# A two-block transformer kernel on one core: a last tile that ends in narrower parts, a norm turned by a diagonal, stand-in products, and an output step moved

## The reference

```python
def rms_norm_2(x, g):
    y = xf * lax.rsqrt(jnp.mean(xf * xf, axis=-1, keepdims=True) + EPS)
    return (y * g.astype(jnp.float32)).astype(x.dtype)
...
def second_block(x, c, ...):
    sh1, sc1, ga1, sh2, sc2, ga2 = jnp.split(mod, 6, axis=-1)
    for _ in range(DEPTH_2):                # DEPTH_2 = 1
        h = modulate(rms_norm_2(x, g_attn), sh1, sc1)
        x = x + ga1[:, None, :] * hybrid_mixer(h, w_in, b_f, sinks, w_out)
        h2 = modulate(rms_norm_2(x, g_mlp), sh2, sc2)
        x = x + ga2[:, None, :] * conv_glu_mlp(h2, w_up, conv_w, conv_b, w_down)
    return rms_norm_2(x, g_final)
```

## Time and profile before

| | us |
|---|---|
| median of three runs | 1611.72 |
| lowest and highest | 1610.78, 1612.98 |
| the profiled execution | 1614.05 |
| its span, first to last instruction | 1612.3 |
| TensorE matmuls busy in it | 1368.0 |
| mean granted TensorE clock | 0.927 of 2.4 GHz |

### The profile page before, as it was taken

One profiled execution on the slowest core, in us unless ns is written; L12 is line 12 of the kernel. 1 busy time (PEld: TensorE's weight loads), 2 busy tenths in 40 slices (PEclk: granted clock), 3 DMA queues, 4 the chain that ended last, 5 costly groups with the idle time before them and its releaser, 6 DMA issues.

```text
span 1612.3 us, 24352 instructions
## 1 busy us (share of the span) xinstructions
PE 1368.0 (85%) x9392; PEld 823.7 (51%) x9392; DVE 561.5 (35%) x1481; ACT 263.1 (16%) x736; POOL 103.6 (6%) x191
## 2 busy tenths in 40 slices
PE   9989998776776877989998768767668999999998
PEld 4445554443433433555654434334335876888843
DVE  3444633221221223552532212212213043577721
ACT  2143211010010011453110100100101133111100
POOL 1312000000000001310100000000001041000000
PEclk9999999898898899999999877988988979999999
DMA  8877999999999999636999999999999621644300
GB/s 295 309 269 278 395 402 421 421 421 422 422 422 422 422 422 391 239 131 239 417 411 420 420 420 420 421 420 420 421 421 353 220 79 42 206 157 155 133 0 26
DMA packets 117190, 512.99 MB, mean 318 GB/s; under 512 B 11872, under 2 KB 46620, under 8 KB 64872
## 3 DMA queue, kind: packets, MB, share of 16 engines
q1 hardware_dynamic: 115376, 507.49, 79.5%
q0 software_dynamic: 1552, 4.06, 0.8%
q10 hardware_dynamic: 168, 0.09, 0.0%
HBM read 510.54 MB, written 1.07 MB: 317 GB/s over the span
## 4 chain that ended last, share of the span: by engine, by line
PE 35%; DMA 12%; SPq 7%; DVE 2%; issue 1%; ACT 1%; POOL 0%; POOLq 0%; DVEq 0%; ACTq 0%
PE bank L2176 9%; DMA ring<-in_moe_w_up 7%; SPq L1634 7%; PE bank L2208 5%; PE bank L1226 4%; DMA BC<-in_moe_w_up 3%; PE bank L1931 3%; PE bank L397 2%; PE bank L409 2%; DMA BC<-in_moe_w_gate 2%; PE bank L1213 1%; PE bank L1241 1%; PE bank L645 1%; PE bank L668 1%; PE bank L502 1%; PE bank L1254 1%
## 5 line engine op out<-in xcount | busy, mean ns | idle before, releaser
L1226 PE MATMUL bank<-ring,hT 128*32 128x256 f32 (+1 forms) x2976 | 304.2, 465 | 153.2 <-DMA ring<-in_moe_w_up 61.0
L1226 PEld LDWEIGHTS bank<-ring,hT 128*32 128x32 f32 (+1 forms) x2976 | 154.9, 134 | 271.2 <-issue 164.1
L1226 PE MATMUL bank<-BC,hT 128*32 128x256 f32 (+1 forms) x1120 | 166.2, 461 | 50.4 <-DMA ring<-in_moe_w_up 26.9
L1485 DVE TENSOR_SCALAR pT<-pT 128x256 f32<-128x256 f32 x34 | 10.0, 294 | 465.5 <-ACT pT L1601 465.5
L2176 PE MATMUL bank<-hT,ring 128*128 128x256 f32 (+1 forms) x768 | 153.0, 362 | 0.0
L2176 PEld LDWEIGHTS bank<-hT,ring 128*128 128x128 f32 x768 | 136.0, 190 | 16.6
L1226 PEld LDWEIGHTS bank<-BC,hT 128*32 128x32 f32 (+1 forms) x1120 | 81.2, 134 | 90.7 <-issue 64.8
L1213 PE MATMUL bank<-A,hn 128*128 128x128 f32 x1088 | 127.2, 275 | 0.0
L502 PE MATMUL bank<-ring,hT 128*128 128x512 f32 (+4 forms) x352 | 123.1, 511 | 4.0 <-DVE hT L300 2.5
L1213 PEld LDWEIGHTS bank<-A,hn 128*128 128x128 f32 x1088 | 124.5, 192 | 1.7 <-issue 1.7
L1254 PE MATMUL bank<-hT,A 128*128 128x512 f32 x256 | 118.4, 605 | 0.0
(11 more groups left out here) (300 smaller groups left out, 1484.8 us busy)
## 6 DMA issues: line engine op xcount, KB each, us to landing
ring<-in_moe_w_up SPq DMA_DIRECT2D x98, 1024.0 KB, 26.6
ring<-in_moe_w_down SPq DMA_DIRECT2D x96, 1024.0 KB, 26.5
ring<-in_moe_w_gate SPq DMA_DIRECT2D x88, 1024.0 KB, 25.7
BC<-in_moe_w_gate SPq DMA_DIRECT2D x40, 1024.0 KB, 24.7
BC<-in_moe_w_up SPq DMA_DIRECT2D x30, 1024.0 KB, 24.1
BC<-in_moe_w_down SPq DMA_DIRECT2D x28, 1024.0 KB, 27.1
ring<-in_w_ada SPq DMA_DIRECT2D x24, 1024.0 KB, 6.7
ring<-in_w_up SPq DMA_DIRECT2D x22, 1024.0 KB, 5.3
```

Source lines behind the costliest of these rows:

```text
L1226: i = nc.tensor.matmul(GATE[q * cap:(q + 1) * cap, part * FF:(part + 1) * FF], xg[:, c, q * cap:(q + 1) * cap], u[:, c, :], start=(c == 0) ...
```

## The change

Four edits.

- The last tile. Tile 1's down product now goes into three parts: 512 columns, then 256, then 256 (in bank 0). Behind each part DVE multiplies by the gate, adds to X, and multiplies the new X by g_final into hn while the root is not there yet. ACT squares 768 columns and then the last 256 (tile 0: 512 and 512); POOL adds both sums in its first instruction; DVE multiplies hn by the root in two halves; SP sends the first half of the tile and ACT the second.
- The norms n3 and n4. DVE no longer scales a whole tile: it scales the 128x128 identity by the roots (into modrow), and PE turns X by a real matmul against that diagonal.
- The third mixer's start. Two matmuls of 512 columns on constants, whose output nobody reads, stand before the turn of tile 0 and two more behind it (keep_warm).
- The first attention's output product: the two pieces of item 8 move behind item 10's transposes of heads.

```diff
@@ norm_stage
             def scale(dve, tt):
-                tile_ready(dve, tt)
                 dve.wait_ge(*rooted(tt + 1))
-                nc.vector.tensor_scalar(hn[:, tt, :], X[:, tt, :], rstd[:, tt:tt + 1], None,
-                                        ALU.mult).then_inc(scaled.sem, 1)
+                nc.vector.tensor_scalar(diagonal_of(tt), ident, rstd[:, tt:tt + 1], None, ALU.mult).then_inc(scaled.sem, 1)
...
+                    if late_root:
+                        i = nc.tensor.transpose(dst, X[:, tt, c:D:DC], ident)
+                    else:
+                        i = nc.tensor.matmul(dst, X[:, tt, c:D:DC], diagonal_of(tt), start=True, stop=True)
@@ close_tensor_short (warm=True for n3 alone)
+            if warm:
+                keep_warm(pe, 7, NB, 2)
             norm.turn(pe, 0)
+            if warm:
+                keep_warm(pe, 7, NB, 2)
+        def keep_warm(pe, b, width, times=1):
+            for _ in range(times):
+                nc.tensor.matmul(bank[b][:, 0:width], ident, konst[:, P:P + width], start=True, stop=True)
@@ OutStage.tensor
-                    counts = (2, 2, 0, 2, 2, 2, 1, 1)
+                    counts = (0, 2, 2, 2, 2, 2, 1, 1)
@@ mlp_tensor
+        parts_of = [[(bank[4], 0, NB), (bank[5], NB, D)],
+                    [(bank[6], 0, NB), (bank[7][:, 0:256], NB, 768), (bank[0][:, 0:256], 768, D)]]
...
+            for tt, together in ((0, parts_of[0]), (1, parts_of[1][0:1]), (1, parts_of[1][1:2]), (1, parts_of[1][2:3])):
@@ mlp_vector
+                    dv.done(nc.vector.tensor_tensor(product, ps, gate_rows[1][:, a:b], ALU.mult))
+                    nc.vector.tensor_tensor(xs, xs, product, ALU.add).then_inc(out_added.sem, 1)
+                    done += 1
+                    dve.wait_ge(*out_added(done))
+                    dv.done(nc.vector.tensor_tensor(hn[:, tt, a:b], xs, g_fin[:, a:b], ALU.mult))
@@ last_scalar
+            for tt, added, a, b in ((0, 1, 0, NB), (0, 2, NB, D), (1, 4, 0, 768), (1, 5, 768, D)):
+                act.wait_ge(*out_added(added))
+                nc.scalar.activation(square_at[:, a:b], X[:, tt, a:b], ACT.Square,
+                                     accum_out=last_ss[:, tt, (a > 0) * 1:(a > 0) * 1 + 1]).then_inc(last_sq.sem, 1)
+            act.wait_ge(*result(4))
+            act.dma_start(out[0, P:S, NB:D], hn[:, 1, NB:D]).then_inc(final_out.sem, 16)
@@ last_scale
+            for n in range(2):
+                y = hn[:, tt, n * NB:(n + 1) * NB]
+                nc.vector.tensor_scalar(y, y, r, D ** 0.5, ALU.mult, ALU.mult).then_inc(result.sem, 1)
@@ sync engine
+            sp.wait_ge(*result(3))
+            sp.dma_start(out[0, P:S, 0:NB], hn[:, 1, 0:NB]).then_inc(final_out.sem, 16)
```

More of the change, by code:

```diff
@@ L249, in norm_stage, with diagonal_of @@
         def norm_stage(tile_ready, gain, shift=None, extra=(), late_root=False):
+            def diagonal_of(tt):
+                return modrow[:, tt * P:(tt + 1) * P]
             st = Stage()
@@ L279, in turn @@
                     pe.wait_ge(*scaled(tt + 1))
-                rows = X if late_root else hn
+                    tile_ready(pe, tt)
                 for c in range(DC):
-                    i = nc.tensor.transpose(bank[4 + 2 * tt + c // 4][:, (c % 4) * P:(c % 4 + 1) * P],
-                                            rows[:, tt, c:D:DC], ident)
+                    dst = bank[4 + 2 * tt + c // 4][:, (c % 4) * P:(c % 4 + 1) * P]
+                    if late_root:
+                        i = nc.tensor.transpose(dst, X[:, tt, c:D:DC], ident)
+                    else:
+                        i = nc.tensor.matmul(dst, X[:, tt, c:D:DC], diagonal_of(tt), start=True, stop=True)
                 i.then_inc(turned.sem, 1)
@@ L342, in close_vector_late, with close_tensor_short @@
             norm.evac(dve, 1, 0)
-        def close_tensor_short(pe, products, norm):
+        def close_tensor_short(pe, products, norm, warm=False):
             for tt in range(TT):
@@ L2196, in mlp_tensor @@
             pe.wait_ge(*cw_out(1))
[L2198 to L2211, removed]
+            for tt, together in ((0, parts_of[0]), (1, parts_of[1][0:1]), (1, parts_of[1][1:2]), (1, parts_of[1][2:3])):
+                for j in range(PAIRS):
+                    u = down_units[j]
+                    if tt == 0:
+                        pe.wait_ge(*hid3(j + 1))
+                        unit_here(pe, u)
+                    w = units[u][0](slot(u))
+                    for c in range(2):
+                        for ps, a, b in together:
+                            i = nc.tensor.matmul(ps, hidT3[:, 2 * j + c, tt * P:(tt + 1) * P], w[:, c, a:b],
+                                                 start=(j == 0 and c == 0), stop=(j == PAIRS - 1 and c == 1))
+                i.then_inc(down_done.sem, 1)
         def mlp_scalar(act):
@@ L2255, in mlp_vector @@
             dve.wait_ge(*fin_in(16))
+            done = 0
             for tt in range(TT):
-                for n in range(2):
-                    dve.wait_ge(*down_done(tt * (n + 1) + 1))
-                    gated(1)(tt, n, bank[4 + 2 * tt + n][:, :]).then_inc(out_added.sem, 1)
+                for k, (ps, a, b) in enumerate(parts_of[tt]):
+                    dve.wait_ge(*down_done(1 if tt == 0 else 2 + k))
+                    xs, product = X[:, tt, a:b], BC[:, 7168 + a:7168 + b]
+                    dv.done(nc.vector.tensor_tensor(product, ps, gate_rows[1][:, a:b], ALU.mult))
[3 more added lines that the diff above has]
+                    dv.done(nc.vector.tensor_tensor(hn[:, tt, a:b], xs, g_fin[:, a:b], ALU.mult))
@@ L2260, in mlp_vector @@
                 last_scale(dve, tt)
-        last_sq, last_rs, result = shared("sum_sq", 2), shared("sum_rs", 2), sem("result")
+        last_sq, last_rs, result = shared("sum_sq", 4), shared("sum_rs", 2), sem("result")
+        last_ss = stat[:, 0:4].rearrange("p (t k) -> p t k", t=TT)
+        square_at = A[:, 2048:2048 + D]
         def last_scalar(act):
[L2266 to L2269, removed]
+            for tt, added, a, b in ((0, 1, 0, NB), (0, 2, NB, D), (1, 4, 0, 768), (1, 5, 768, D)):
[4 more added lines that the diff above has]
+            act.dma_start(out[0, P:S, NB:D], hn[:, 1, NB:D]).then_inc(final_out.sem, 16)
@@ L2298, in _ @@
             load(m2_units[1], len(units))
[L2299 to L2302, removed]
+            sp.wait_ge(*result(2))
+            sp.dma_start(out[0, 0:P, :], hn[:, 0, :]).then_inc(final_out.sem, 16)
+            sp.wait_ge(*result(3))
+            sp.dma_start(out[0, P:S, 0:NB], hn[:, 1, 0:NB]).then_inc(final_out.sem, 16)
+            sp.wait_ge(*final_out(16 * 3))
         @block.gpsimd
```

15 lines of the change are left out of this document (7 added, 8 removed).

## The result

| | before | after |
|---|---|---|
| median, us | 1610.19 (6 runs) | 1618.24 (6 runs) |
| lowest and highest | 1608.05, 1612.98 | 1616.45, 1621.96 |
| the profiled execution | 1614.05 | 1621.96 |
| its span | 1612.3 | 1620.1 |
| TensorE matmuls busy in it | 1368.0 | 1383.4 |

A forecast was written before the change was run, and what follows sets the result against it. TensorE, busy 1368.0 of 1612.3 us, was taken to bound the kernel, with an unoverlapped tail behind it. Tail -2.0, n4 +1.8, n3 -1.4 and first attention +0.2 gave -1.4 us: 1610.3 us, range 1607.6 to 1613.1.

The forecast's parts named there:

- The price of a turn: n4: 16 real-matmul instructions at 0.112 us take 1.79 us against 0.88 for eight transposes, 0.91 more for each turn.
- The bounds I gave: n4's two turns: +1.6 if a turn's start is hidden, +2.2 us if a hand-over is exposed at each turn.
- the sum of -1.4: Whole kernel: tail -2.0, n4 +1.8, n3 -1.4 and first attention +0.2 make -1.4 us.
- n4: +1.8 forecast: n4's two turns lie in TensorE's gapless run, so their longer real matmuls are paid in full: +1.8 us.
- n3: -1.4 forecast: Third mixer's start: faster matmuls at full clock, half given back to longer turns and tile 1's root: -1.4 us.
- The credit for the clock: n3: with idle time filled the clock stays at 1.00, twelve matmuls take 2.6 us instead of 5.4.
- The rival with the short fall: n3: without a profile before's clock fall is short, so n3 is worth -0.1 us, giving 1611.6; chance 0.15.
- The first attention: +0.2 forecast: Item 8 without the pieces: TensorE idles about 0.25 us longer awaiting ACT's copy, same work at half clock: +0.2 us.
- a second one comes: First attention's upper bound: a second half-clock stretch, since the pieces no longer cover item 8's hand-over to ACT: +1.6 us.
- The tail: -2.0 forecast: Behind the last matmul: narrower steps, smaller square, split final scaling and two transfers save 2.0 us.
- The rival that gave this to ACT's queue: Tail: ACT's transfer as late as the whole tile was, tail only -1.0 us, 1611.3 in all; chance 0.10.
- The rival for slower by over 3.2 us: Whole kernel: several rivals at once and a stall not seen here, slower by over 3.2 us; chance 0.03.

The follow-up runs named there:

- the last tile alone: Before with only the new last tile (512 + 256 + 256 columns, early g_final, two halves out), also called the tail alone: 1609.49 us, 1.0002.
- the turn alone: Before with only the real matmul against the diagonal of roots in n3 and n4, nothing else of the change: 1618.31 us, 1.0054.
- stand-ins alone: Before with only the four keep_warm matmuls on constants around n3's first turn, transposes kept: 1610.46 us, 1.0000.
- the turn with contiguous columns: Before with only the real-matmul turn, reading 128 neighbouring columns of X (computes another function): 1611.12 us, 1.0008.
- four kernels with the same last steps: New last tile on before: by itself 1.0002, with keep_warm 0.9998, all edits but the real-matmul turn 0.9991, the latter with SP sending both halves 0.9985.

## Why the prediction failed

**The price of a turn: the step that failed.** For n4, "real products of 128 columns are two instructions each, and 32 of those take 3.57 us, 0.112 each: 16 take 1.79". The two instructions are right, and the 0.112 is right for the earlier trace rows, whose stationary operand lies without gaps. The turn's stationary operand is X at every eighth element. In before's turns the operand has the same gaps, and there eight transposes take 0.88 us with loads of 0.188 to 0.191 us. The data is what these load, too: a weight load's shape in the trace is that of the transposed data and not that of the identity, as in the turn of 44x128 rows against an identity of 44x44 (L2171). And before's transposes of contiguous columns (L656) load faster than its gapped ones:

```profile
L656 PEld LDWEIGHTS bank<-konst,BC x96: 137/141/230, 100.8 to 1354.5; 128*128 128x128 f32 x96
L2171 PEld LDWEIGHTS bank<-konst,BC x4: 136/138/139, 1374.7 to 1374.8; 44*128 44x128 f32 x4
L2171 PE MATMUL bank<-konst,BC x4: 232/233/256, 1374.7 to 1374.9; 44*128 44x44 f32 x4
```

So the gapped slice is the stationary operand before and after. A transpose's load takes 0.141 us without gaps and 0.188 with them; a real matmul's takes 0.192 without and 0.336 with. Why the gaps cost the real matmul 0.144 us and the transpose 0.047 no run here tells. But that they cost something at all stood in the trace of before. The bounds I gave, +1.6 to +2.2, had both been taken within this one reading of the row, so the range couldn't hold what came. No row that the forecast used has a gapped stationary operand in a real matmul; the price was therefore unknown, and was treated as known to 0.2 us for each turn.

Put the measured turns, 3.87, 4.03, 3.69 and 3.82 us, in place of the forecast's 1.8, 1.8, 1.79 and 1.79, and the sum of -1.4 becomes -1.4 + 15.4 - 7.2 = +6.8. The spans of the profiled executions differ by +7.8, the medians by +8.05. One term was mis-sized, and it entered four times.

**n4: +1.8 forecast, +5.7 measured.** The mechanism was right: both turns lie in TensorE's gapless run, and every microsecond arrived at the end. With contiguous columns the turns took exactly what was forecast.

**n3: -1.4 forecast, +2.7 measured.** Three of its steps came: the granted clock stays at 1.00 in every kernel that has the stand-ins, the twelve matmuls take 2.91 us (2.6 forecast), and the second turn's first load waits for tile 1's root. The two turns add 4.3 us to what was forecast, and -1.4 + 4.3 = +2.9 meets the measured +2.7 to 0.2. The credit for the clock, though, was the price of one execution. Before's fall at n3 lasts 6.8 us, that of the last tile alone, which idles the same, 3.4, and with the turn alone TensorE idles 1.49 and 1.71 us and the clock doesn't fall at all. So against the turn alone the stand-ins gave after nothing, and against before their ratio alone is 1.0000. The rival with the short fall, at 0.15, had the right idea of this. Where no fall would have come, the stand-ins should cost about nothing, by the rows: from the end of the last product to the first turn it is 2.04 us with them and 2.03 without, to the twelve matmuls 4.90 and 4.89 (stand-ins alone against before). That is an estimate; no execution with transposes, without stand-ins and without a fall was seen.

**The first attention: +0.2 forecast, +1.2 in the profiled execution, nothing that can be told in the ratio.** The wait is 2.42 us and not 2.14, and is ended by ACT's copy, as forecast; after's row:

```profile
120.50 1.22 PE L681 MATMUL bank<-A,pT 128*128 128x128 f32 x4 [2.42 <-ACT pT L792]
```

What made it 1.2 is the clock, in after for 6.8 us instead of 3.4 (before: the earlier trace rows):

```profile
118.00:120.50 2.50, 0.09 (x2) 0.01 (x1) 1.31 (x7) 1.30 (x5) 0.73 (x2) 0.95 1.01 419
120.50:127.00 6.50, 6.50 (x16) 3.56 (x17) 2.51 (x9) 2.86 (x13) 1.48 (x5) 0.50 1.01 425
```

But before and eight of the kernels, with the moved pieces or without, show a fall of 3.4 us there, and the turn alone and the turn with contiguous columns, whose first attention is before's to the instruction and idles the same 2.14 us, show none; the row of the turn alone for 118 to 128:

```profile
118.00:128.00 10.00, 8.22 (x40) 4.80 (x40) 5.51 (x23) 5.80 (x24) 2.31 (x6) 1.00 1.01 424
```

So the same program there has a fall in one execution and none in another, and the moved pieces have one of 6.8 us in after and of 3.4 in four other kernels: the length of a fall goes with the execution and not with the edit. The bound of "a second one comes" was +1.6, and 1.2 lies in it.

**The tail: -2.0 forecast, -1.75 measured, -0.8 in four kernels with the same last steps.** The steps in DVE, ACT and POOL are what was forecast to 0.1 us (0.42, 0.42, a square of 0.42, 0.88 for both halves), and 6.23 us against the "about 6.0" named ahead. The term that varies is the landing of the second half: 2.2 us were taken (0.4 less than the big transfer's 2.6), and it came to 2.3 in after and to 3.2 where the thin rest comes. The rival that gave this to ACT's queue was near in the size for the kernels with the rest (-1.0 against -0.8), not for after, and wrong in the cause. Neither size shows in the ratios of the tail alone, 1.0002 ± 0.0012: an edit of 0.8 to 1.75 us is below what 12 runs tell here.

**The sign.** The rival for slower by over 3.2 us stood at 0.03 as "several of these at once and a stall not seen here". It should have been one mechanism with a price, and much of what it needed was in the trace: all four turns of n3 and n4 are on the chain, and the gapped loads took 0.188 us where contiguous ones took 0.141. The point from which it decides was near. From -1.4 to +3.2 it is 4.6 us, 1.15 for each turn, 0.072 for each of its 16 instructions: at 0.184 us for one and not 0.112 the change is slower by over 0.2%. It came to 0.24.

## What to carry to other kernels

A duration taken from another row is only as good as its operands' access: before a transpose is replaced by a real matmul, look at how far apart the columns of the stationary operand lie, for a gap that costs a transpose's weight load little (0.047 us here) can cost a real matmul's three times as much and set the pace. Where an edit repeats on the critical path, the widest bound belongs to its unit price and not to the sum. And a stretch at half clock in one profiled execution is not a gain that can be booked in full: compare two or three executions before it is given a price.

## What the runs showed of the hardware

- The weight load of a real float32 matmul, 128 columns, takes 0.192 us with columns 1 element apart, 0.196 with 2, 0.329 with 4 and 0.335 with 8. A turn of 16 such loads and matmuls takes 2.06, 2.09, 3.61 and 3.81 us. The forecast had no dependence on the distance.
- The same slice in a transpose against the identity is the stationary operand too, has loads of 0.188 us, and eight of those transposes take 0.88 us. Contiguous columns load in 0.141 us in a transpose.
- A transfer of 256 KB issued 0.4 us behind another one lands after 2.3 us in two profiled executions and 3.2 in three, on ACT's queue; with both on SP's the median of the two is 2.7. The first lands after 2.0 in all of those where it can be read alone.
- In the first attention, behind an idle time of 2.14 us the granted clock falls to 0.50 for 3.4 us in five profiled executions and stays at 1.00 in two; behind 2.42 us the fall lasts 3.4 us in four and 6.8 in one. The Trainium skill ("TensorE: Matmul & The Clock Gate", Part 1) calls the clock run-variable where it tells of a kernel's start; here the same shows in the middle of a kernel.
